# Two-layer transformer with MoE on one Trainium2 core: the first modulation pair ahead of the tokens, the token rows scaled on ScalarE, and unit 0's blocks one place later

## What is computed

```python
def rms_norm(x):
    xf = x.astype(jnp.float32)
    return (xf * lax.rsqrt(jnp.mean(xf * xf, -1, keepdims=True) + NORM_EPS)).astype(x.dtype)

def modulate(x, shift, scale):
    return rms_norm(x) * (1 + scale[:, None, :]) + shift[:, None, :]

def swiglu(u, w_gate, w_up, w_down):
    return (jax.nn.silu(u @ w_gate) * (u @ w_up)) @ w_down

c_act = jax.nn.silu(c)
mod = c_act @ w_ada[l] + b_ada[l]
sh1, sc1, g1, sh2, sc2, g2, sh3, sc3, g3 = jnp.split(mod, N_MOD, axis=-1)
x = x + 0.5 * g1[:, None, :] * swiglu(modulate(x, sh1, sc1), ffn1_gate[l], ffn1_up[l], ffn1_down[l])
```

## Time and profile before

| | |
|---|---|
| median of three runs | 1729.2 us |
| the three runs | 1728.34, 1729.2, 1733.05 us |
| the profiled execution | 1731.83 us, its span 1730.1 us |
| mean granted TensorE clock | 0.993 |
| PE, DVE, ACT busy | 97%, 78%, 57% of the span |
| HBM read | 435.36 MB, 252 GB/s over the span |

### The profile page before, as it was taken

One profiled execution on the slowest core, in us unless ns is written; L12 is line 12 of the kernel. 1 busy time (PEld: TensorE's weight loads), 2 busy tenths in 40 slices (PEclk: granted clock), 3 DMA queues, 4 the chain that ended last, 5 costly groups with the idle time before them and its releaser, 6 DMA issues.

```text
span 1730.1 us, 24793 instructions
## 1 busy us (share of the span) xinstructions
PE 1682.9 (97%) x8505; PEld 1387.3 (80%) x8512; DVE 1353.3 (78%) x2093; ACT 989.2 (57%) x1551; POOL 47.0 (3%) x92
## 2 busy tenths in 40 slices
PE   6999999999999999999999999999999999999998
PEld 4888888888788878887888888888887877888886
DVE  6887877758776678788777578878778579999997
ACT  4444565755644464445656565445646567777775
POOL 0000000000000000000000000000000000000000
PEclk9999999999999999999999999999999999999999
DMA  8898863235676758887632348988473626999994
GB/s 366 337 350 325 346 232 125 98 110 182 255 278 244 274 191 320 327 300 289 236 106 98 134 171 316 346 326 319 177 269 118 242 99 243 375 352 355 371 352 161
DMA packets 61803, 437.43 MB, mean 253 GB/s; under 512 B 6816, under 2 KB 7328, under 8 KB 9504
## 3 DMA queue, kind: packets, MB, share of 16 engines
q1 hardware_dynamic: 47360, 338.44, 51.6%
q0 software_dynamic: 12672, 92.28, 14.7%
q10 hardware_dynamic: 1696, 5.72, 0.9%
HBM read 435.36 MB, written 1.05 MB: 252 GB/s over the span
## 4 chain that ended last, share of the span: by engine, by line
PE 87%; DVE 5%; ACT 4%; DMA 2%; issue 1%; SPq 0%; DVEq 0%; ACTq 0%
PE bank L2116 25%; PE bank L2118 25%; PE bank L2117 25%; PE bank L2415 2%; DMA raw<-weight_stream 1%; DMA arena<-ada_pairs 1%; PE bank L2436 1%; PE bank L2245 1%; PE bank L2448 1%; PE bank L2395 1%; PE bank L2153 1%; ACT w_hi L536 1%; DVE arena L1215 1%; PE bank L2389 1%; PE bank L2393 0%
## 5 line engine op out<-in xcount | busy, mean ns | idle before, releaser
L536 ACT ACTIVATE w_hi<-raw 128x1024 fp32r<-128x1024 f32 x394 | 395.3, 1054 | 293.7 <-PE bank L2118 276.0
L2116 PE MATMUL bank<-w_hi,uT_hi 128*128 128x512 f32 (+1 forms) x1384 | 540.7, 391 | 16.7 <-DVE uT_lo L1620 5.7
L1126 DVE TENSOR_TENSOR w_lo<-raw,w_hi 128x1024 fp32r<-128x1024 f32 x388 | 457.0, 1221 | 96.4 <-ACT w_hi L536 95.2
L2117 PE MATMUL bank<-w_lo,uT_hi 128*128 128x512 f32 (+1 forms) x1384 | 527.8, 381 | 0.0
L2118 PE MATMUL bank<-w_hi,uT_lo 128*128 128x512 f32 (+1 forms) x1384 | 527.6, 381 | 0.0
L2116 PEld LDWEIGHTS bank<-w_hi,uT_hi 128*128 128x128 f32 x1384 | 261.6, 189 | 74.0 <-issue 7.9
L2118 PEld LDWEIGHTS bank<-w_hi,uT_lo 128*128 128x128 f32 x1384 | 261.2, 189 | 51.0
L2117 PEld LDWEIGHTS bank<-w_lo,uT_hi 128*128 128x128 f32 x1384 | 261.8, 189 | 45.5
L1158 DVE CUSTOM_DVE_ANT_0 ada_w<-ada_w,cmpw 128x1024 f32<-128x1024 f32 x176 | 207.8, 1221 | 8.9 <-DMA ada_w<-ada_pairs 8.9
L2116 PE MATMUL bank<-w_hi,r_arena 128*128 128x512 f32 (+1 forms) x392 | 155.6, 397 | 4.2 <-DVE r_arena L2013 2.5
L2118 PE MATMUL bank<-w_hi,r_arena 128*128 128x512 f32 (+1 forms) x392 | 151.7, 387 | 0.0
(11 more groups left out here) (378 smaller groups left out, 1961.8 us busy)
## 6 DMA issues: line engine op xcount, KB each, us to landing
raw<-weight_stream SPq DMA_DIRECT2D x216, 1024.0 KB, 6.4
ada_w<-ada_pairs POOLq DMA_DIRECT2D x88, 1024.0 KB, 5.3
raw<-expert_blocks SPq DMA_DIRECT2D x48, 1024.0 KB, 4.9
ada_w<-expert_blocks SPq DMA_DIRECT2D x32, 1024.0 KB, 4.9
cmpw<-expert_blocks SPq DMA_DIRECT2D x16, 1024.0 KB, 5.1
arena<-ada_pairs SPq DMA_DIRECT2D x5, 1024.0 KB, 13.4
ada_w<-ada_pairs SPq DMA_DIRECT2D x3, 1024.0 KB, 13.6
cmpw<-compress_w ACTq DMA_DIRECT2D x2, 1024.0 KB, 14.0
```

The source lines that it names most:

```text
L536: act.activation(w_hi[:, b], v, ACT.Copy).then_inc(hi_done, 1)
L1126: V.tensor_tensor(w_lo[:, b], v, f32(w_hi[:, b]), ALU.subtract).then_inc(split_done, 1)
L2116: pe.matmul(dst, xh, hi, start=first, stop=False, skip_group_check=True)
L2117: pe.matmul(dst, xh, lo, start=False, stop=False, skip_group_check=True)
```

## The change

Three things are changed, all of them ahead of the feed-forward loop:

- SP issues pair 0 ahead of the tokens and constants, pair 1 ahead of `vec`, and each of unit 0's blocks 0 and 1 behind one more pair.
- VectorE sums both halves of pair 0 before it waits for the tokens, and no longer scales the rows of `xn`.
- ScalarE scales them instead, with the function that later norms already use (`scale`, four activations of 128 by 512), between the second root and `first_hi(0)`.

```diff
-            sp.dma_start(c_bc, c_rows[0]).then_inc(c_landed, 16)
-            sp.dma_start(x[:, :, :], x_in.rearrange("(t p) d -> p t d", p=P)).then_inc(x_landed, 16)
-            sp.dma_start(cst[:, 0:K_DIST], consts[:, 0:K_DIST]).then_inc(cst_landed, 16)
-            for st, pair in enumerate(FIRST_ORDER):
+            def load_pair(st):
                 slot = st % len(first_w)
                 if st >= len(first_w):
                     sp.wait_ge(ada_done, st - len(first_w) + 1)
-                sp.dma_start(first_w[slot], ada[pair]).then_inc(first_landed[slot], 16)
-                if st == 0:
-                    sp.dma_start(vec[:, :], vecs).then_inc(vec_landed, 16)
-                if st in (1, 3):
-                    load_unit0(st // 2)
+                sp.dma_start(first_w[slot], ada[FIRST_ORDER[st]]).then_inc(first_landed[slot], 16)
+
+            sp.dma_start(c_bc, c_rows[0]).then_inc(c_landed, 16)
+            load_pair(0)
+            sp.dma_start(x[:, :, :], x_in.rearrange("(t p) d -> p t d", p=P)).then_inc(x_landed, 16)
+            sp.dma_start(cst[:, 0:K_DIST], consts[:, 0:K_DIST]).then_inc(cst_landed, 16)
+            load_pair(1)
+            sp.dma_start(vec[:, :], vecs).then_inc(vec_landed, 16)
+            load_pair(2)
+            load_unit0(0)
+            for st in range(3, 6):
+                load_pair(st)
+            load_unit0(1)
+            for st in range(6, len(FIRST_ORDER)):
+                load_pair(st)
             load_unit0(2)
...
             for t in range(T):
                 squares(0, t)
                 root(0, t)
+            for t in range(T):
+                scale(0, t)
...
             V.memset(mods_step[:, :], 0.0).then_inc(mods_kept, 1)
+            dve.wait_ge(c_ready, 1)
+            first_pair(0)
             dve.wait_ge(x_landed, 16)
             V.memset(eps, EPS).then_inc(x_ready, 4)
-            dve.wait_ge(c_ready, 1)
             rms_sum(0, 0)
-            first_pair(0, (0,))
             rms_inverse(0, 0)
-            rms_scale(0, 0)
             rms_sum(0, 1)
-            first_pair(0, (1,))
             rms_inverse(0, 1)
-            rms_scale(0, 1)
             dve.wait_ge(vec_landed, 16)
```

## The result

| | before | changed |
|---|---|---|
| median | 1729.93 us | 1733.97 us |
| lowest and highest of nine | 1728.34 to 1733.05 us | 1731.7 to 1736.96 us |
| ratio of the medians, 95% interval | | 1.0023, 1.0014 to 1.0032 |
| profiled execution, span | 1731.83, 1730.1 us | 1731.7, 1729.7 us |

The change costs 4.0 us here: inside the predicted range and inside 0.3%, but more than the 1.5 us of the forecast. Three comparisons of the changed kernel stand in this document; their ratios are 1.0023, 1.0015 and 1.0019, each with an interval that leaves out 1, and the differences of the means are 4.4, 2.5 and 2.7 us. Over all 31 executions of it and 93 of the kernel before, the means are 1733.74 and 1730.76 us: **+3.0 us, 95% interval about 0.7 to either side**.

What follows compares the result with a forecast made beforehand. TensorE bounds most of the kernel, but the start hangs on VectorE's list up to its fourth split. First split 2.05 us late less pair 4's 0.53 gives +1.5, from 1729.2 to 1730.7 us; range 1728.0 to 1734.4.

Steps and rivals of the forecast that it cites:

- The queue: Transfers at the start: block 0, now eighth, lands at pair 2's old time, 17.95 us instead of 15.5.
- The first split: VectorE at the start: waits 2.3 us for ScalarE's copy of block 0, splits at 19.2, 2.05 us late.
- Pair 4's wait: VectorE's list at the start: the 0.53 us of waiting for pair 4 come back, as it lands at 22.9.
- The rope: Start of the program: whatever moves VectorE's fourth split moves the rest by as much; +1.5 us, down product at 56.6.
- The rival that the delay would be absorbed: Between fourth split and first down product: weights and PE win back the 1.5 us; 1729.2 us, chance 0.14.
- the forecast path: From the fourth split: it frees a place in `raw`, SP issues a block, copy and split precede the down product.
- The rival by which the relief on VectorE wins: VectorE at the start: block 0's copy is there in time, so -0.8 us, 1728.4 us; chance 0.15.
- The scalings: ScalarE ahead of block 0's copy: four scalings, 2.9 us at most, covered by the wait and costed at nothing.
- The size of the sum: Fourth split and whole program: 2.05 - 0.53 = +1.5 us, no measurable change forecast.
- the bound of +2.2: Upper bound of the whole shift, if the 0.53 us return as another wait and the transposes are slow.
- anything under 5.2: Whole-kernel measurement: claimed to tell a difference from none at about 0.3%, or 5.2 us.
- The rival with three additional falls: TensorE's clock falls more often in gaps between stages: 1.5 + 3 x 1.7 = 6.6 us, 1735.8 us; chance 0.05.

Runs made afterwards that it cites:

- the three pairs above: Kernels differing by the scalings' place alone: changed, changed with pair 2 summed ahead of the first split, kernel before; ScalarE slower by means by 1.4, 1.3, 0.5 us.
- the larger dose: Changed kernel with unit 0's block 0 two places later again in the queue, behind pair 4: 1737.47 us (six executions), ratio 1.0044.

## Why the prediction was right, and where it was not

**The queue: right.** "The first eight are again the same eight, so block 0, now eighth, lands at pair 2's old time": 17.63 where 17.95 was forecast. `cst` is there at 9.8 (10.2), pair 0 at 7.0 (7.7). All came 0.3 to 0.7 us earlier than forecast. The shift of the blocks alone gives the same copy time, and two more transfers give 5.1 us more, 2.55 per MB (forecast from the trace: 2.5).

**The first split: right, 0.45 us too late.** Forecast 19.2 with 2.3 us of idleness, measured 18.75 with 2.44. VectorE was free 0.6 us earlier than I thought: pair 1 began at 13.66, not 14.3, mostly because `cst`, and the squares behind it, came 0.4 to 0.5 us earlier. The rest is the row statistics, which took less than the 0.8 us given to them. That only made the wait longer. "What the moved pair and the lifted scalings save is nearly used up by the later constants" was wrong by this 0.6 us, and without effect.

**Pair 4's wait: right.** It is gone, and where the blocks are put back it returns. One correction to the description of the change: block 1 went behind two more pairs (4 and 5), not one. ScalarE waits 0.4 us for it, but its copy begins at 27.6 us and the third split, at 31.92, doesn't wait.

**The rope: right at the start.** Fourth split +1.0 (forecast 1.5; 38.57 and 38.59 in the other two profiles), SP's next block at 39.91, first down product at 56.42, 56.15 and 56.48 (56.6). In all twelve profiles the down product starts 17.6 to 17.9 us behind the fourth split, whether that stands at 36.63 or at 43.61. The rival that the delay would be absorbed there is out.

But the path between the two is not always the forecast one. By it the freed place lets SP issue a block, whose split releases the down product, as before. In this profile of the changed kernel, the timeline of VectorE has that split, and the timeline of TensorE has no wait in front of the product:

```profile
53.63 2.35 DVE L1135 TENSOR_TENSOR w_lo<-raw,w_hi 128x1024 fp32r<-128x1024 f32 x2
```

```profile
36.09 0.50 PE L2122 MATMUL bank<-w_hi,uT_hi 128*128 128x512 f32 x1 [1.83 <-DVE uT_lo L1629]
...
56.42 0.39 PE L2122 MATMUL bank<-w_hi,hT_hi 128*128 128x512 f32 x1
```

The weights are there at 55.98 us (53.63 + 2.35), and before the change the product started 0.15 us behind them (54.96 to 55.11). Here it started 0.44 us behind them, because TensorE, working without a pause since 36.09, was itself late: its clock had fallen from 36 to 41 us. So the forecast path moved the down product by 1.0 us (54.96 to 55.98), and the additional fall of the clock gave 0.3 more. In the second profile of the changed kernel, which lacks that fall, the product starts 0.15 us behind the weights again (56.00 to 56.15). The 16 matmuls on zeros took 5.08 us and not 6.54, so the transposes ended at 16.7 us instead of 19, without effect.

The rival by which the relief on VectorE wins is out too: it had no time to win even with the blocks at their old place, because pair 4 binds in its stead.

**The scalings: here a step failed.** "The wait covers them and I cost them at nothing." On the start's path it does cover them. But there are costs that no wait covers. First, the time of an execution outside its span: in the profiled ones 1.96 to 2.02 us in all five kernels that scale on ScalarE (here 1731.7 against a span of 1729.7), 1.67 to 1.73 in the four others (1731.83 against 1730.1; 1727.67 against 1726.0): +0.3. The other executions bear it out: 1.95 to 2.06 us in every one of the first kind, 1.62 to 1.73 in every one of the second. Second, a stretch in the experts, 1.6 ms behind the edit. ACT in the kernel before, at the end:

```profile
1655.35 2.01 ACT L565 ACTIVATE w_hi<-raw 128x1024 fp32r<-128x1024 f32 x2 [0.44 <-PE bank L2118]
```

and in the changed kernel's third profile:

```profile
1654.00 2.01 ACT L572 ACTIVATE w_hi<-raw 128x1024 fp32r<-128x1024 f32 x2 [0.72 <-PE bank L2124]
```

The same copy, with 0.28 us more idleness before it. All twelve profiles have one value or the other: 0.44 us in the five with the scalings on VectorE, 0.72 in the seven with them on ScalarE. From the last table load (1443.62 before, 1441.95 here) the copy lies 211.7 to 211.8 us off in the five, 211.9 to 212.05 in the seven, and nothing behind it makes that up: from that load to the end of the span are 286.5 to 286.6 us in the five and 286.8 to 286.9 in the seven. So +0.25. Together 0.55 us, which agrees with the +0.4 us by means of the two kernels whose fourth split comes when it did before and whose scalings are on ScalarE; but a mean of theirs is uncertain by over 1 us, so these two times alone would not have shown it; the traces do, and the average of the three pairs above (1.1 us, uncertain by 0.7) agrees. What causes the two costs was not tried, only that they come with the scalings on ScalarE. The Trainium skill (ScalarE: Activation LUTs, Rules for kernel authors) wants multiplications on VectorE, for the time per element. The durations agree (0.64 us against 0.44 apiece), but the wait covered them; what the move cost here are the two terms above.

**The size of the sum.** Forecast 1.5 us, measured 3.0, with 0.7 to either side: above the bound of +2.2 that the prediction gave for the shift. The 1733.97 us lie in the predicted range through the room it left for scatter, 0.4 us under its upper end; that part is luck. And a difference of 3 us was no longer lost in the measurement, as the prediction had it for anything under 5.2: all three intervals leave out 1. From the traces I can find: the start, +1.1 to +1.3 (the table load behind it at 213.33, 213.61 and 213.44 against 212.57 and 212.05; the down product); around the span +0.3; in the experts +0.25. That makes 1.7 to 1.9. **The rest, 1.1 to 1.3 us, the traces do not locate.** Part of it can be the clock: each execution's result has its mean granted clock, and within one kernel 0.001 less of it goes with 1.0 us more. The changed kernel's executions average 0.9937 and those of the kernel before 0.9941, which makes 0.4 us, uncertain by 0.5. At the same granted clock the difference would be 2.6 us, with 0.5 to either side, and 0.7 to 0.9 us stay open. The rest is no multiple of the delay (the larger dose cost no more than its own delay). The parts add up as far as the scatter lets one say: +2.05 for the blocks alone and +0.4 for the scalings alone make 2.5. It may be scatter in part.

**The clock.** The rival with three additional falls didn't come. The start of the changed kernel has two in some profiles (0.76 from 21 to 28 us, 0.66 from 36 to 41), and its down product lies 0.3 us behind that of the profile with one (56.42 and 56.48 against 56.15). Later in the program a fall comes or stays away in one and the same kernel, at 360 us worth 1.5 us (forecast 1.7).

## What to carry to other kernels

In a full queue the place of a transfer is its time: work out which bytes lie ahead of it, and before moving it back, ask whether the engine that wants it has other work until then. If it hasn't, as here, put that work there in the same edit: summing a pair ahead of the split took the whole 2.4 us of wait away, and the fourth split came 1.9 us earlier. And two profiled spans that differ by a few microseconds in 1700 say nothing on an edit at the start; compare the same instruction's time at fixed places behind it, and look at the granted clock between them.

## What the runs showed of the hardware

- **Time around the span depends on the program**: 1.7 us or 2.0 us, the same to 0.1 us in every execution of a kind, with four more ScalarE and four fewer VectorE instructions in the second kind. Which of the two counts, or what it stands for, was not tried.
- **Small stalls without a releaser**: the last `uT_lo` started 0.54 us after the rounding that it is said to wait for, and 2.39 to 2.40 us behind the split instead of 1.96, in the kernels whose VectorE list is four instructions shorter ahead of it. The profile names a releaser (`uT_hi`) that had long been done. What it was stays open. A second such place is the copy in the experts, 0.44 us or 0.72 behind its wait, by kind of kernel.
- **The clock's falls are not fixed to the program**: executions of the changed kernel had spans from 1728.8 to 1733.3 us with the same start to 0.35 us. At 360 us the grant was 1.00 once and 0.83 another time.
